# Per-head sums of squares on two column quarters of PE, with a spread matrix of 128 rows

## The reference

```python
def rms_norm(x, g):
    xf = x.astype(jnp.float32)
    y = xf * lax.rsqrt(jnp.mean(xf * xf, axis=-1, keepdims=True) + RMS_EPS)
    return (y * g.astype(jnp.float32)).astype(x.dtype)

def l2_normalize(x):
    return x * lax.rsqrt(jnp.sum(x * x, axis=-1, keepdims=True) + NORM_EPS)
...
    q = l2_normalize(to_heads(q)) * (HEAD_DIM ** -0.5)
    k = l2_normalize(to_heads(k))
...
    o = o * lax.rsqrt(jnp.mean(o * o, axis=-1, keepdims=True) + NORM_EPS) * norm_w.astype(jnp.float32)
```

## Time and profile before

| | |
|---|---|
| three runs | 2901.48, 2901.95, 2916.73 us (median 2901.95) |
| the profiled execution, device time | 2897.08 us |
| its span, first to last instruction | 2895.3 us |
| PE busy / weight loads busy | 2766.1 us (96%) / 2617.9 us (90%) |
| DVE / ACT / POOL busy | 1810.6 us (63%) / 1249.2 us (43%) / 201.9 us (7%) |
| mean granted clock of PE | 0.980 of full speed |
| read from memory | 541.48 MB, 188 GB/s over the span |

### The profile page before, as it was taken

One profiled execution on the slowest core, in us unless ns is written; L12 is line 12 of the kernel. 1 busy time (PEld: TensorE's weight loads), 2 busy tenths in 40 slices (PEclk: granted clock), 3 DMA queues, 4 the chain that ended last, 5 costly groups with the idle time before them and its releaser, 6 DMA issues.

```text
span 2895.3 us, 50110 instructions
## 1 busy us (share of the span) xinstructions
PE 2766.1 (96%) x22070; PEld 2617.9 (90%) x22070; DVE 1810.6 (63%) x2229; ACT 1249.2 (43%) x1375; POOL 201.9 (7%) x202
## 2 busy tenths in 40 slices
PE   6899989998999999989999999998999999999998
PEld 3599877787988998889999999888899999999998
DVE  2347877677777545557555555696656675466753
ACT  4333334444543334435444436544444444344444
POOL 0001101010000000002132130003000000000000
PEclk9899999998999999999999999999999999999999
DMA  9756655574776554435555554440245555555554
GB/s 370 314 181 226 227 182 186 205 252 162 242 252 227 196 189 175 160 139 186 175 175 172 171 175 149 146 175 16 88 160 194 200 186 192 202 192 190 194 191 139
DMA packets 90984, 546.81 MB, mean 189 GB/s; under 512 B 10608, under 2 KB 10768, under 8 KB 45840
## 3 DMA queue, kind: packets, MB, share of 16 engines
q1 hardware_dynamic: 69552, 466.39, 45.3%
q0 software_dynamic: 18432, 67.12, 6.9%
q10 hardware_dynamic: 2784, 10.11, 0.9%
HBM read 541.48 MB, written 2.10 MB: 188 GB/s over the span
## 4 chain that ended last, share of the span: by engine, by line
PE 66%; DVE 6%; ACT 2%; issue 2%; ACTq 0%; DVEq 0%
PE bank L725 66%; DVE r L2150 2%; ACT r L1457 1%; DVE f L2720 1%; PE bank L785 1%; DVE f L2784 0%; ACT f L1819 0%; DVE f L2781 0%; DVE f L2797 0%; DVE f L2532 0%; DVE f L2186 0%; DVE f L2773 0%; DVE f L2549 0%; ACT L1807 0%; DVE r L2555 0%
## 5 line engine op out<-in xcount | busy, mean ns | idle before, releaser
L725 PE MATMUL bank<-r,r 128*128 128x256 f32 (+1 forms) x19596 | 2423.2, 286 | 46.9 <-DVE r L2150 21.0
L725 PEld LDWEIGHTS bank<-r,r 128*128 128x128 f32 x19596 | 2355.3, 190 | 103.0 <-DVE r L2150 29.8
L2150 DVE TENSOR_TENSOR r<-f,r 128x2048 fp32r<-128x2048 f32 (+2 forms) x447 | 959.8, 2148 | 723.8 <-ACT r L1457 721.1
L1457 ACT CAST r<-f 128x2048 fp32r<-128x2048 f32 (+2 forms) x447 | 793.3, 1777 | 865.6 <-PE bank L725 657.2
L725 PE MATMUL bank<-f,f 128*128 128x128 f32 (+10 forms) x1992 | 328.1, 378 | 56.2 <-DMA f<-in_units 22.5
L725 PEld LDWEIGHTS bank<-f,f 128*128 128x128 f32 (+3 forms) x1992 | 219.8, 177 | 119.9 <-issue 52.6
L2186 DVE SCALAR_TENSOR_TENSOR f<-f,f,f 128x512 f32<-128x512 f32 x240 | 180.0, 750 | 27.8 <-DMA f<-in_later 18.9
L2720 DVE SCALAR_TENSOR_TENSOR f<-f,f,f 128x255 f32<-128x255 f32 (+1 forms) x272 | 134.0, 495 | 8.8
L1474 ACT COPY f<-bank 128x512 f32<-128x512 f32 x149 | 83.9, 584 | 108.1 <-PE bank L725 102.3
L3045 POOL DMA_DIRECT2D f<-in_later x128 | 67.8, 529 | 872.1 <-DVE f L2186 713.6
L3054 POOL TENSOR_TENSOR f<-f,f 32x512 f32<-32x512 f32 x24 | 61.7, 2570 | 664.2 <-DVE f L2658 664.2
(11 more groups left out here) (235 smaller groups left out, 921.7 us busy)
## 6 DMA issues: line engine op xcount, KB each, us to landing
f<-in_units SPq DMA_DIRECT2D x346, 1024.0 KB, 4.8
f<-in_units SPq DMA_DIRECT2D x124, 768.0 KB, 4.3
f<-in_later POOLq DMA_DIRECT2D x128, 512.0 KB, 4.6
f<-in_units SPq DMA_DIRECT2D x8, 576.0 KB, 5.0
f<-in_x ACTq DMA_DIRECT2D x2, 1024.0 KB, 12.8
f<-in_ctx ACTq DMA_DIRECT2D x2, 1024.0 KB, 11.9
f<-in_x_turned ACTq DMA_DIRECT2D x1, 2048.0 KB, 11.7
out<-f SPq DMA_DIRECT2D x4, 256.0 KB, 4.0
```

The costliest lines, as they stand in the source:

```text
L725: return e.matmul(o, lhsT, rhs, start=start, stop=stop, skip_group_check=True)
L1457: e.copy(unit_view(high[HIGH_OF[u]][1], u), unit_view(raw[RAW_OF[u]][0], u)).then_inc(*up("w_hi", ("hi", u)))
L2150: e.tensor_tensor(unit_view(raw[RAW_OF[u]][1], u), unit_view(raw[RAW_OF[u]][0], u), unit_view(high[HIGH_OF[u]][1], u).bitcast(F32), ALU.su ...
```

## The change

The sums of even tiles now go to rows 0 to 31 of the bank and those of odd tiles to rows 32 to 63: the stationary matrix is 32 columns wide, and column i // 2 of it is ones for tile i, so that tile i lands in row 32 * (i % 2) + i // 2, and the other rows get zeros added. Each tile's matmul keeps its wait and its semaphore step. The root, the reciprocal and the two parts are made on 64 rows in place of 8, the high part lies in rows 64 to 127 of `hrr`, and `spread` has 128 rows with ones in the two rows of each head. All rows of `hrr` are now written, so the copy of zeros is gone. `pick` grows from 64 to 128 columns of the block of constants that is loaded at the start. Tiles behind it in SBUF move by 64 bytes.

```diff
-    pick = np.zeros((128, 64), np.float32)
+    pick = np.zeros((128, 128), np.float32)
+    for x in range(4):
+        pick[:, 32 * x + x] = 1.0
+    spread = np.zeros((128, 1024), np.float32)
     for h in range(8):
-        pick[:, 8 * h + h] = 1.0
-    spread = np.zeros((40, 1024), np.float32)
-    for h in range(8):
-        spread[h, 128 * h:128 * h + 128] = 1.0
-        spread[32 + h, 128 * h:128 * h + 128] = 1.0
+        for row in (32 * (h % 2) + h // 2, 64 + 32 * (h % 2) + h // 2):
+            spread[row, 128 * h:128 * h + 128] = 1.0
...
-        cs, hr = cs[0:32, :, :], cs[32:40, 0, :]
+        cs, hr = cs[0:32, :, :], cs[64:128, 0, :]
...
-                mm(e, o[0:8, 0:T], C["pick"][:, 8 * i:8 * i + 8], tmps[i % len(tmps)][:, 0:T], i == 0, i == tiles - 1).then_inc(
+                row, x = 32 * (i % 2), 32 * (i // 2)
+                mm(e, o[row:row + 32, 0:T], C["pick"][:, x:x + 32], tmps[i % len(tmps)][:, 0:T], i < 2, i >= tiles - 2).then_inc(
...
-                ins = mm(e, o[:, x * T:(x + 1) * T], spread[0:40, h * 128:(h + 1) * 128], hrr[0:40, slot, :], x == 0, True)
+                ins = mm(e, o[:, x * T:(x + 1) * T], spread[:, h * 128:(h + 1) * 128], hrr[:, slot, :], x == 0, True)
...
-            e.activation(hr, ps("hrs", name)[0:8, 0:T], ACT.Sqrt, bias=eps[0:8, :], scale=scale).then_inc(
+            e.activation(hr, ps("hrs", name)[0:64, 0:T], ACT.Sqrt, bias=eps[0:64, :], scale=scale).then_inc(
...
-            e.tensor_copy(hrr[32:40, slot, :], hr).then_inc(*up("dve_norm"))
+            e.tensor_copy(hrr[64:128, slot, :], hr).then_inc(*up("dve_norm"))
...
-            e.tensor_tensor(hrr[0:8, slot, :], hr, hrr[32:40, slot, :].bitcast(F32), ALU.subtract).then_inc(
+            e.tensor_tensor(hrr[0:64, slot, :], hr, hrr[64:128, slot, :].bitcast(F32), ALU.subtract).then_inc(
...
-            e.tensor_copy(hrr[0:40, :, :], C["spread"][64:104, 0:3 * T].rearrange("p (a b) -> p a b", a=3)).then_inc(*up("dve_norm"))
-            e.tensor_copy(spread[0:40, :], C["spread"][0:40, :]).then_inc(*up("dve_norm"))
+            e.tensor_copy(spread[:, :], C["spread"]).then_inc(*up("dve_norm"))
```

More of the change, by code:

```diff
@@ L25 @@
 SLAB = 53132
-KEEP = 9360
+KEEP = 9376
 ALPHA = 4.0 ** 0.25
```

## The result

The change makes the kernel **slower**: 2972.69 us (median of 4 runs, 2969.21 to 2974.89) against 2902.73 (4 runs, 2901.48 to 2916.73), a ratio of 1.0225 with the interval [1.0176, 1.0273], which lies clear of 1 and reaches to both sides of 2%. The forecast was 2896.8 us within 2888 to 2907, so it missed by 76 us, and the range missed too. The profiled execution took 2974.89 us, its span is 2973.1 us.

The account below looks back on a forecast made before the run. PE, busy for 96% of the span, was taken as the bound. 0.78 + 1.74 + 1.73 + 1.06 - 0.10 = 5.2 us off the runs' median of 2901.95 gave 2896.8 us, range 2888 to 2907.

Parts of the forecast that it names:

- What is added or costs nothing: Side costs: 64 rows and the dropped zero copy cost or gain nothing; loading 32 KB more constants costs 0.1 us.
- should step at 0.115 us throughout: Sign to look for: plain products in the stretch with the spreading step at 0.115 us, no 40-row products left.
- slower rival: PE's clock falls behind waits, at the "dlk" and "dlq" bursts and following units; five long falls give 2913.8 us; chance 0.10.
- the waits eat it: DVE and ACT chains behind "dlk" and before the attention absorb savings; only "osum" passes on, 1.9 us, 2900.0; chance 0.15.
- Price of a pair: Two tiles side by side take 0.64 us for 1.03; eight tiles in a burst 1.89 us, saving 1.73.
- The middle of "qb": Second and third pair of "qb", 2.13 us for eight passes: ACT's squares decide, so nothing is saved.
- "dlk" ends with ACT: The "dlk" burst now ends with ACT's last square, at 1830.07 in place of 1830.94, saving 0.87 us.
- 128 rows in the spreading: Spreading products get the plain shape, so switches of about 0.2 us each way go; 1.06 us taken in all.
- 64 rows for DVE and ACT: Root, reciprocal and two parts on 64 rows in place of 8 take no longer; nothing taken.
- The second pass stands in the way: Strict program order of passes: "osum" takes nine steps, not eight; saving 4.6 us, 2897.4; chance 0.10.
- The change does not do what it says: Semaphore steps or waits keep pairs one behind another; only the spreading's saving stays, 1.0 us, 2901.0; chance 0.08.
- All of PE's saving counts: Every pair and every island of 40-row products counts in full: 11.8 us saved, 2890.1; chance 0.07.

Follow-up runs that it names:

- e1: Kernel before with KEEP 9376 in place of 9360 and nothing else, so tiles lie 64 bytes higher as in the change: 2975.56 us, 1.0225 of the kernel before.
- e3: Kernel after with only the weights' buffers 64 bytes higher, giving back the old distance of 192: 2895.89 us, 0.9954 of the kernel before.
- e12: Kernel after, unchanged, run once more beside a version with serial sums: 2968.99 us (6 runs).
- e6: Kernel after with the tiles moved by another 256 bytes, distance 0 modulo 256: 2969.40 us.
- e5: Kernel after with the tiles moved by another 192 bytes, distance 192 modulo 256: 2893.53 us.
- e14: Not the layer: products of zeros, PE alone, long stretches at distances 0 to 480 bytes, then short ones behind thin products; 22.01 us at 320 bytes.
- e9: Kernel after with only the buffers of the weights' high parts 64 bytes higher, mixing distances 192 and 0: 2945.40 us, 1.0145 of the kernel before.

## Why the prediction was wrong, point by point

**The step that failed.** The part "What is added or costs nothing" priced the larger block of constants by its transfer alone, 0.1 us, and had no term for where it pushes what lies behind. That the tiles move by 64 bytes stood in the text on the change, and I gave it no price. The sum then took the plain step of 0.115 us as fixed on both sides, and the sign that it named ("should step at 0.115 us throughout") is the one that came out wrong: 120.0 ns. The missing term measured 77.3 us in the groups by shape, fifteen times the sum. The range had no case for it either. Its slower rival had PE's clock fall; it ended at 2913.8 us, and it was not that: the mean granted clock is 0.979 after and 0.980 before, and 1.00 in both windows of the MLP.

**The steps that held, and one that did not.** At equal placement, e1 against after, each instance can be timed in the two timelines, from the start of its burst to the same later row:

| piece | e1, us | after, us | saved | the sum had |
|---|---|---|---|---|
| "qb": first pair to DVE's reciprocal | 22.24 | 21.37 | 0.87 | 0.78 |
| "dlk": burst to the end of the spreading | 29.59 | 28.09 | 1.50 | 0.87 + 0.61 |
| "dlq": burst to the work behind the spreading | 21.38 | 19.80 | 1.58 | 0.87 + 0.25 |
| "osum": unit ahead to the unit behind | 29.79 | 27.91 | 1.88 | 1.73 + 0.20 |

That is 5.8 us, where the sum had 5.3 for these four. In the last three, what was saved stays: from the plain stretch ahead of "dlk" to PE's last row it is 1114.13 us in e1 (1842.70 to 2956.83) and 1109.84 after (1853.56 to 2963.40), 4.29 us less. "dlq" differs in size: with slower products PE came to it late, with no wait ahead of the burst, so the squares bound it less. In e3, at the old distance, PE waits 0.60 us ahead of it, and from the burst to the same later row it takes 20.27 us where the kernel before took 21.05: 0.78 us saved for 1.12, since the wait for DVE behind the spreading grew from 4.34 to 4.67. There, then, a part of what the burst lost went into the next wait, as the rival "the waits eat it" had it.

"qb" is a second step that failed, small beside the first. Its 0.87 us reach DVE's reciprocal, and the prediction took them as passed on from there to the attention. On the way DVE adds up a later layer's modulation (line 2187, 2186 in e1), whose operands come by a transfer of their own, and it waits for that for 0.94 and 2.13 us after, for 0.45 and 0.74 in e1. The first row is the longest of these waits; then come PE's first rows of the attention that wait for DVE, after and in e1:

```profile
373.40 1.54 DVE L2187 SCALAR_TENSOR_TENSOR f<-f,f,f 128x512 f32<-128x512 f32 x2 [2.13 <-DMA f<-in_later]
...
380.94 1.09 PE L785 MATMUL bank<-f,f 128*128 128x128 f32 x4 [5.82 <-DVE f L2377]
```

```profile
380.08 0.63 PE L785 MATMUL bank<-f,f 128*128 128x128 f32 x4 [2.40 <-DVE f L2377]
```

Counted from the first pair of "qb" (285.90 and 285.88 us), PE goes on at 95.04 us after and at 94.20 in e1: 0.84 us later, where the sum had 0.78 sooner. In e12, the same kernel again, it is 94.90, and in e6 93.81: what arrives changes from run to run by more than the term. So of the sum's 5.3 us for the four some 4.3 are left behind the bursts of these two traces. Their whole spans cannot be compared for 5 us: after has 2973.1 us and e1 2966.5, since after falls behind by 11 us in waits between 360 and 750 us, and e12, the same kernel (2963.7), by 5.

- *Price of a pair.* The passes of a pair in "osum" start 6 or 7 ns apart and the next pair 0.216 us later: the step taken. 1.92 us was measured for 1.89.
- *The middle of "qb".* The second and third pair take from 298.15 to 300.21 us, 2.06 us in place of 2.13, with a wait of 0.50 us for ACT between them: next to nothing saved, as argued.
- *"dlk" ends with ACT.* ACT's last square and PE's burst after, from the timelines of ACT and PE: 1866.42 + 2.56 = 1868.98, and PE ends at 1866.98 + 2.67 = 1869.65, 0.67 us behind it, where 0.75 were written.

```profile
1866.42 2.56 ACT L1591 ACTIVATE f<-f 128x256 f32<-128x256 f32 x8
```

- *128 rows in the spreading.* The stretch behind the wait in "dlk" takes 12.71 us for 104 products, where e1, with its rows of 40, takes 13.29: 0.58 us for 0.61.
- *64 rows for DVE and ACT.* DVE's reciprocal took 1.75 us in place of 1.74, as taken. Its start was not sooner by the clock of the trace, since all products ahead of it were slower:

```profile
307.27 1.75 DVE L2306 RECIPROCAL f<-f 64x256 f32<-64x256 f32 x1 [1.53 <-ACT f L1617]
```

**The rivals.** "The second pass stands in the way" would have made "osum" nine steps, 2.11 us; at 1.92 it falls: the second tile's first pass starts 6 or 7 ns behind the first tile's, and ahead of the first tile's second pass. The Trainium skill states a strict order of start and end ("TensorE: Matmul & The Clock Gate", section "The mechanism"). In this trace whole matmuls start in order, and the first tile's last pass too starts 6 ns ahead of the second's, but single passes do not keep to it. The semaphore steps of the pairs left little: 0.03 us in that burst, and 0.04 behind it, since ACT's root starts 0.07 us behind PE's last pass (at 2102.20 + 1.92 = 2104.12) where it was 0.03:

```profile
2104.19 0.47 ACT L1617 ACTIVATE f<-bank,f 64x256 f32<-64x256 f32 x1 [5.34 <-PE bank L725]
```

The Trainium skill ("TensorE: Matmul & The Clock Gate", section "The cost: per-tile semaphore tail") would have added some 0.2 us, an estimate from its 26.3 ns for each of eight. "The change does not do what it says" falls with the table above. "The waits eat it" is right for "qb" in both traces of the kernel after, and for 0.3 us of "dlq" at the old distance, and wrong for the rest. "All of PE's saving counts" falls with "qb".

**The change at the old distance.** e3 and e5 have the change and the old distance: 0.9954 [0.9921, 0.9988] and 0.9975 [0.9944, 1.0006] of the kernel before. The first is clear of 1 by little, the second is not. The forecast of 5.2 us, 0.9982, lies in both intervals, but these are over 0.6% wide and say little of 0.2% (the kernel before ran from 2891.28 to 2928.33 us in the series of e3). That the sum was about that of a kernel in which the tiles stay where they were, modulo 256 bytes, rests on the pieces in the traces.

**What stays open.** That the reads of moving tiles and the loads of weights disturb each other is the reading that fits: only their distance counts, PE alone shows it, and both moved together show nothing. What in the chip they meet at, and why a stretch takes one rhythm and not the other, no run shows. Other types and widths of product were not tried.

## What to carry to other kernels

A change that grows a constant or a buffer moves everything behind it, and that can cost more than the edit earns: list which operands move against which, and compare the step of an untouched stretch (here the 96 plain products at "qb", 11.17 us or 11.78) before looking at the lines that changed. Where a kernel is bound by a stream of matmuls with a new stationary matrix for each, sweep the distance between its two operands over 256 bytes in a program of a few hundred products, and pad so that edits cannot shift it. And test an edit at equal placement, or its own worth drowns: some 4 us of gain stood here against 77 of shift.

## What the runs showed of the hardware that was not expected

- The step of a 128 x 128 by 256 float32r product, each with a load of weights, depends on the start distance of the two operands modulo 256 bytes. Alone, from the rows of e14 as (us - 0.28) / 191, the longer first steps of a stretch in it: 120.4 ns at 0, 117.1 at 32, 113.7 at 64, 120.4 at 96, 119.1 at 128, 117.7 at 160, 113.8 at 192, 118.7 at 224. PE's busy share (100%) and the granted clock (1.00) are the same in the windows of before and after; the count of products is not.
- One distance can have two rhythms, 113.3 and 117.8 ns in the short stretches of e14 at 192 bytes; which one a stretch takes changed with what ran just ahead of it.
- Products of two distances in one stream share a step between the two (117.8 ns in e9) in place of keeping their own.
- Two-pass matmuls on two column quarters run pass beside pass: in "osum" the passes of a pair start 6 or 7 ns apart, and eight tiles take 1.92 us in place of 3.62.
- Transfers at 326 to 395 GB/s, or ACT and DVE fully busy, left these steps as they were.
